# A hybrid recurrence and expert layer: the seam between a gated recurrence and a row projection rearranged (split early row, store awaited later, value splits placed sooner, four landing places)

## What is computed

```python
px = split(u_x @ w_in)                 # q, k, v, gate of group A; q, two z, v, gate of group B
ret = bidirectional_scan(q, k, v, fixed decays)          # group A: retention, 4 heads
f   = lb + (1 - lb) * sigmoid(z)                         # group B: HGRN2 recurrence, 4 heads
hg  = bidirectional_scan(silu(q), 1 - f, v, log f)
a = rms(ret) * silu(gate_a);  b = rms(hg) * w * silu(gate_b)
y = concat([a, b]) @ w_out
h = x + g1 * y                         # g1 and five other rows come from silu(c) @ w_ada + b_ada
out = rms(h + g2 * experts(...)) * norm_final_w
```

## Time and profile before

| what | us |
|---|---|
| time, median of three runs | 2895.38 |
| the profiled execution: its own time | 2889.01 |
| the profiled execution: span of the trace | 2887.3 |
| PE busy in the span | 2683.8 (93%) |
| DVE busy | 2034.6 (70%) |
| ACT busy | 1440.6 (50%) |
| mean granted TensorE clock | 0.965 of full speed |

### The profile page before, as it was taken

The page is one execution under the profiler, slowest core; times in us unless marked ns, Lnnn a source line. Parts: engine busy times, 40 slices in busy tenths (PEclk is TensorE's granted clock), DMA queues, the critical chain, the costliest instruction groups (busy, mean ns, idle before and its releaser), DMA issues. The chain is left out here.

```text
span 2887.3 us, 38466 instructions
## 1 busy us (share of the span) xinstructions
PE 2683.8 (93%) x13003; PEld 2124.9 (74%) x13004; DVE 2034.6 (70%) x2211; ACT 1440.6 (50%) x1471; POOL 510.9 (18%) x437
## 2 busy tenths in 40 slices
PE   7999999799679499999999999999999999999994
PEld 3668677477568387777787787888878877787773
DVE  3566666570666597899969878766686678967884
ACT  4433535320634375677747556544454446645653
POOL 0424434200002221112202111101111111111110
PEclk9999999899789699999999999999999999999997
DMA  6101100170233697899959878676586678968873
GB/s 254 30 23 30 30 23 15 65 257 1 95 117 83 245 351 264 283 360 358 362 197 350 297 243 315 229 251 201 189 285 203 215 269 298 343 204 278 283 242 131
DMA packets 266131, 596.65 MB, mean 207 GB/s; under 512 B 21356, under 2 KB 46612, under 8 KB 264944
## 3 DMA queue, kind: packets, MB, share of 16 engines
q1 hardware_dynamic: 245680, 552.56, 53.6%
q0 software_dynamic: 20384, 43.19, 6.7%
HBM read 577.75 MB, written 42.25 MB: 215 GB/s over the span
## 5 line engine op out<-in xcount | busy, mean ns | idle before, releaser
L2041 DVE TENSOR_TENSOR e_slot_r<-e_slot,whi 128x2048 fp32r<-128x2048 f32 x296 | 674.5, 2285 | 128.1 <-ACT whi L1983 128.1
L1983 ACT ACTIVATE whi<-e_slot 128x2048 fp32r<-128x2048 f32 x296 | 561.1, 1912 | 374.3 <-PE e_acc L1894 374.3
L1892 PE MATMUL e_acc<-whi,e_xhi 128*128 128x512 f32 x1600 | 631.3, 395 | 0.5
L1894 PE MATMUL e_acc<-whi,e_xlo 128*128 128x512 f32 x1600 | 628.4, 393 | 0.0
L1983 ACT ACTIVATE whi<-slot 128x2048 fp32r<-128x2048 f32 x148 | 283.1, 1913 | 186.2 <-PE e_acc L1894 186.2
L2041 DVE TENSOR_TENSOR slot_r<-slot,whi 128x2048 fp32r<-128x2048 f32 x151 | 345.0, 2287 | 19.9 <-ACT whi L1983 17.2
L1894 PEld LDWEIGHTS e_acc<-whi,e_xlo 128*128 128x128 f32 x1600 | 300.0, 187 | 70.6
L1892 PEld LDWEIGHTS e_acc<-whi,e_xhi 128*128 128x128 f32 x1600 | 301.1, 188 | 67.2 <-DVE e_slot_r L2041 4.2
L1892 PE MATMUL e_acc<-whi,e_ahi 128*128 128x512 f32 x800 | 320.4, 400 | 0.0
L1893 PE MATMUL e_acc<-slot_r,e_xhi 128*128 128x512 f32 x800 | 314.6, 393 | 0.0
L1894 PE MATMUL e_acc<-whi,e_alo 128*128 128x512 f32 x800 | 313.6, 392 | 0.0
(11 more groups left out here) (299 smaller groups left out, 3846.3 us busy)
## 6 DMA issues: line engine op xcount, KB each, us to landing
e_slot<-in_w SPq DMA_DIRECT2D x296, 1024.0 KB, 6.6
slot<-in_w SPq DMA_DIRECT2D x151, 1024.0 KB, 6.2
rv<-in_w_ada SPq DMA_DIRECT2D x32, 512.0 KB, 4.7
slot<-in_w_in SPq DMA_DIRECT2D x20, 512.0 KB, 4.1
wa<-in_w_ada SPq DMA_DIRECT2D x8, 1024.0 KB, 16.2
slot<-in_w_in SPq DMA_DIRECT2D x6, 1024.0 KB, 9.2
xt<-in_x SPq DMA_DIRECT2D x8, 512.0 KB, 16.9
slot<-in_w_out SPq DMA_DIRECT2D x4, 1024.0 KB, 14.1
```

Source lines behind the costliest of these rows:

```text
L1892: pe.matmul(out, hi[:, k, c], wh, start=False, stop=False)
L1894: return pe.matmul(out, lo[:, k, c], wh, start=False, stop=last)
L1983: act.activation(whi[i % RING][:], raw[i % PIECES][:], ACT.Copy).then_inc(S["whi_made"], 1)
L2041: v.tensor_tensor(wlo[i % PIECES][:], raw[i % PIECES][:], whi[i % RING][:].bitcast(F32), ALU.subtract).then_inc(S["wlo_made"], 1)
```

## The change

In `hgrn2`: `early_rows` takes the range of weight pieces to do. The last one is done in two halves on PE, with `output(h, 7)` between them; on ACT its copy moves behind `roots(h, 1)`. The buffer `o` is allocated ahead of `val` and `gate`. The store's semaphore becomes one that outlives the stage (`merged_out`), and the wait at the end of SP's list goes.

In `project_retention`: four landing places in place of five, one chunk further into `rv`, so that `rv` tiles 0 and 1 are free of them. ACT waits for the stores to have landed before it writes the high part of the second half of the value weights, and waits for the 32 adds ahead of value tile 2 in place of tile 0. DVE splits the value weights behind `low_rows(4)` and `low_rows(5)`.

```diff
+        o = t.sb("h_o", [P, LT, P])
         val = [t.sb(f"h_val{i}", [P, NT, P]) for i in range(2)]
         gate = t.sb("h_gate", [P, LT, P])
-        o = t.sb("h_o", [P, LT, P])
...
-                sp.dma_start(dram["merged"]..., o[:]).then_inc(S["o_out"], 16)
+                sp.dma_start(dram["merged"]..., o[:]).then_inc(keep["merged_out"], 16)
...
             store(HEADS - 2)
             store(HEADS - 1)
-            sp.wait_ge(S["o_out"], 16 * HEADS)
...
-            def early_rows(x):
+            def early_rows(x, which=range(KT)):
                 n = GROUPS * HEADS + x
-                if x < 2:
+                if which[0]:
+                    pass
+                elif x < 2:
                     group_read(pe, n - 2)
...
-                for k in range(KT):
+                for k in which:
...
-                mm.then_inc(S["rows_done"], 1)
+                if k == KT - 1:
+                    mm.then_inc(S["rows_done"], 1)
...
                 else:
-                    early_rows(3)
+                    early_rows(3, range(KT // 2))
                 if now:
                     output(h, LT - 1)
+                if not more:
+                    early_rows(3, range(KT // 2, KT))
...
                 if not more:
                     early_rows(2)
-                    early_rows(3)
...
                 if now:
                     roots(h, 1)
+                if not more:
+                    early_rows(3)
...
-                v.wait_ge(S["o_out"], 16 * h)
+                v.wait_ge(keep["merged_out"], 16 * h)
...
-        land = [keep["rv"][:]...[:, i * D:(i + 1) * D] for i in range(5)]
+        LANDS = 4
+        land = [keep["rv"][:]...[:, (i + 1) * D:(i + 2) * D] for i in range(LANDS)]
...
-                if n >= 5:
-                    sp.wait_ge(S["ada_added"], n - 4)
-                sp.dma_start(land[n % 5], ...).then_inc(ada_in[n % 5], 16)
+                if n >= LANDS:
+                    sp.wait_ge(S["ada_added"], n - LANDS + 1)
+                sp.dma_start(land[n % LANDS], ...).then_inc(ada_in[n % LANDS], 16)
...
-            for n in range(5):
+            for n in range(LANDS):
                 load_ada(n)
...
                 act.wait_ge(w_in[i], 16 * ((2 * n + half) // SLOTS + 1))
+                if (n, half) == (1, 1):
+                    act.wait_ge(keep["merged_out"], 16 * HEADS)
                 act.activation(whi[i][:], slots[i][:], ACT.Copy).then_inc(S["w_high"], 1)
...
-                if n == 1:
-                    act.wait_ge(S["ada_added"], CHUNKS)
                 if n == 2:
                     act.wait_ge(S["row_summed"], 1)
                 for i in range(first, end):
                     x = BASE[n] + i - first
+                    if n == 1 and i == 2:
+                        act.wait_ge(S["ada_added"], CHUNKS)
...
                 low_rows(i)
-                if i in (7, 8):
-                    low(1, i - 7)
+                if i in (4, 5):
+                    low(1, i - 4)
                 for _ in range(3):
                     add_ada(added)
```

More of the change, by code:

```diff
@@ L379, in hgrn2 @@
         cumulated keys_ready pool_sub exped dec_ready turned ktok_ready u_done states lev_sum lev_sub lev_exp lev_mul lev_ready s_done
-        picked st_ready o_done squared root_ready o_ready o_out rows_done rows_taken""".split()
+        picked st_ready o_done squared root_ready o_ready rows_done rows_taken""".split()
         S = {x: t.sem("h_" + x) for x in names}
@@ L413, in store @@
                 sp.wait_ge(S["o_ready"], LT * (h + 1))
-                sp.dma_start(dram["merged"].rearrange("(i p) n -> p i n", p=P)[:, :, (HEADS + h) * P:(HEADS + h + 1) * P], o[:]).then_inc(S["o_out"], 16)
+                sp.dma_start(dram["merged"].rearrange("(i p) n -> p i n", p=P)[:, :, (HEADS + h) * P:(HEADS + h + 1) * P], o[:]).then_inc(keep["merged_out"], 16)
             sp.dma_start(masks[:].rearrange("p a b -> p (a b)"), dram["masks"]).then_inc(S["const_in"], 16)
@@ L908, in project_retention @@
         acc = keep["rg"][:].rearrange("p i n -> p (i n)")
-        land = [keep["rv"][:].rearrange("p i n -> p (i n)")[:, i * D:(i + 1) * D] for i in range(5)]
-        ada_in = [t.sem(f"p_ada_in{i}") for i in range(5)]
+        LANDS = 4
+        land = [keep["rv"][:].rearrange("p i n -> p (i n)")[:, (i + 1) * D:(i + 2) * D] for i in range(LANDS)]
+        ada_in = [t.sem(f"p_ada_in{i}") for i in range(LANDS)]
         CHUNKS = 4 * KT
@@ L920, in load_ada @@
                 k, c = divmod(n, 4)
-                if n >= 5:
-                    sp.wait_ge(S["ada_added"], n - 4)
-                sp.dma_start(land[n % 5], wa[:, k, (2 + c) * D:(3 + c) * D]).then_inc(ada_in[n % 5], 16)
-            for n in range(5):
+                if n >= LANDS:
+                    sp.wait_ge(S["ada_added"], n - LANDS + 1)
+                sp.dma_start(land[n % LANDS], wa[:, k, (2 + c) * D:(3 + c) * D]).then_inc(ada_in[n % LANDS], 16)
+            for n in range(LANDS):
                 load_ada(n)
@@ L929, in _ @@
                 load_row_weights(sp, dram, keep, 1, half)
-            for n in range(5, CHUNKS):
+            for n in range(LANDS, CHUNKS):
                 load_ada(n)
@@ L1013, in add_ada @@
                 a = acc[:, c * D:(c + 1) * D]
-                v.wait_ge(ada_in[n % 5], 16 * (n // 5 + 1))
+                v.wait_ge(ada_in[n % LANDS], 16 * (n // LANDS + 1))
                 if k == 0:
-                    v.tensor_scalar(a, land[n % 5], sc[:, 0, k:k + 1], None, ALU.mult).then_inc(S["ada_added"], 1)
+                    v.tensor_scalar(a, land[n % LANDS], sc[:, 0, k:k + 1], None, ALU.mult).then_inc(S["ada_added"], 1)
                 else:
                     v.wait_ge(S["ada_added"], n - 3)
-                    v.scalar_tensor_tensor(a, land[n % 5], sc[:, 0, k:k + 1], a, ALU.mult, ALU.add).then_inc(S["ada_added"], 1)
+                    v.scalar_tensor_tensor(a, land[n % LANDS], sc[:, 0, k:k + 1], a, ALU.mult, ALU.add).then_inc(S["ada_added"], 1)
             low_rows(0)
@@ L2208, in build @@
             ident=m.sb("ident", [P, P]), const_in=m.sem("const_in"),
-            lb=m.sb("lb", [P, 8]), oml=m.sb("oml", [P, 8]), lb_ready=m.sem("lb_ready"), emptied=m.sem("emptied"), bound_part=m.sem("bound_part"), u_ready=m.sem("u_ready"), w_out_in=[m.sem(f"w_out_in{i}") for i in range(SLOTS)], hg_in=m.sem("hg_in"),
+            lb=m.sb("lb", [P, 8]), oml=m.sb("oml", [P, 8]), lb_ready=m.sem("lb_ready"), emptied=m.sem("emptied"), bound_part=m.sem("bound_part"), u_ready=m.sem("u_ready"), w_out_in=[m.sem(f"w_out_in{i}") for i in range(SLOTS)], hg_in=m.sem("hg_in"), merged_out=m.sem("merged_out"),
             w_in=[m.sem(f"w_in{i}") for i in range(PIECES)], nw_in=m.sem("nw_in"),
```

## The result

The changed kernel takes 2875.16 us (median of six runs, 2872.30 to 2880.13); the kernel before, run beside it, 2890.78 us (median of six). The ratio is 0.9946, with a 95% interval of 0.9935 to 0.9958: 15.6 us less, 0.54%. The forecast was 15.2 less; the three runs known then had a median of 2895.38, 4.6 above that of the six, so the forecast time of 2880.2 lies 5 us above the measured one, inside the range. The forecast gave 0.45 to more than 0.5% faster and 0.52 to less; 0.54% with an interval from 0.42 to 0.65 doesn't decide between the two.

A forecast was written before the change was run, and what follows sets the result against it. PE, busy for 93% of the span, was taken to set the pace. Gains of 3.44 + 2.79 + 8.93 = 15.16 us, taken from the three-run median of 2895.38, gave 2880.2 us; range 2869 to 2889.

The forecast's parts named there:

- Last output between the halves: End of the recurrence: the output starts sooner, with half of the last early row's products behind it; gain 3.44 us.
- Store awaited later: Boundary to the projection stage: first load 0.80 us behind the store's issue in place of 3.59; gain 2.79 us.
- Rival 2: Boundary to the projection: the barrier holds until the store has landed; gain 12.4 us, time 2883.0; chance 0.08.
- Value splits sooner: Projection's value weights: two PE pauses (5.4 us) and the slow clock behind them (about 3.5) go; gain 8.93 us.
- Rival 1: Behind the two value-weight pauses: the clock fall was that execution's own; gain 11.7 us, time 2883.7; chance 0.20.
- the pauses at 216 and 331: Two equal PE pauses of 2.21 us: clock stayed at 1.00 behind the first, fell to mean 0.62 behind the second.
- Rival 3: DVE late for `low_rows(5)`, 1.0 us of cover: a delay of 3 to 6 us gives 2881 to 2885; chance 0.09.
- Four places and later wait as guards: Projection's adds: they end near 636.2, PE wants them at 643.3, cover 7.1 us; protects the gain, adds none.
- Rival 4: Projection: four places starve the adds, slower than before; gain used up at 9.0 us per load; chance 0.03.
- Clock at the start: PE's slow stretch behind the seam, 5.6 us, worth 2.8: change between +1 and -1 us, taken as 0.
- Later stages: Stages behind the projection start at a barrier and move as a whole.
- Rival 5: Later stages' clock and DMA fall differently and take back 5 us or more: 2885 to 2890; chance 0.05.

The follow-up runs named there:

- e1: Kernel before with only the last output between the halves of the last early row and ACT's copy behind the root; 2886.94 us, ratio 0.9994.
- e6: Changed kernel with ACT's copy of the last early row back ahead of squares and root; one execution, 2879.65 us.
- e2: Kernel before with only the store awaited later, on a semaphore that outlives the stage; ratio 0.9993.
- e4: Changed kernel with the value splits back behind `low_rows(7)` and `low_rows(8)`; ratio 0.9978.
- e11: Changed kernel with both value splits behind `low_rows(4)`; one execution, 2878.19 us.
- e3: Kernel before with only the value splits behind `low_rows(4)` and `low_rows(5)`, keeping five landing places and the old wait; ratio 0.9990.
- e5: Changed kernel with two landing places in place of four; 2896.51 us, ratio 1.0024 against the kernel before.
- e12: Changed kernel with three landing places in place of four; one execution, 2880.60 us.
- e13: Changed kernel with high products first in the first tile, 8 idle PE products ahead of the projection's first wait, 6 more ending the recurrence; ratio 0.9960.
- e9: Changed kernel with 16 idle products on PE ahead of the projection's first wait; ratio 0.9948 against the kernel before.
- e10: Changed kernel with high products first in the first tile and 8 idle PE products ahead of the projection's first wait; ratio 0.9939.

## Why the prediction was right

- *Last output between the halves*: 3.44 expected, 3.43 in e1 and in the changed kernel. That ACT's move is needed holds (e6); that it is worth nothing by itself was not run. Its price if left out was 3.9, not 3.4, as the copy's own 0.6 us had been left out.
- *Store awaited later*: 2.79 expected, 2.82 measured. Rival 2, that the barrier holds until the landing, has fallen (e2). The 512 KB ahead of the first loads cost nothing: from the first load to the first product 5.34 us pass, before 5.35.
- *Value splits sooner*: 8.93 expected; e4 against the changed kernel gives 82.38 - 73.40 = 8.98. Rival 1, that the clock's 3.5 us were one execution's own, has fallen: eight pauses of eight in four profiles were followed by 0.50. The forecast's sum, not the lower bound from the pauses at 216 and 331, was right. The prediction had also weighed a mean gain inside the interval from 11.7 to 15.2; in these four profiles it lay at the upper end. Nor were the unequal ends of those two pauses mostly chance: in all 14 profiles the clock fell behind the one in the place of 331, and in 4 behind the one in the place of 216, so the place counts, and why stays open. Rival 3 did not happen, but its cover was 1.0 us as stated (e11); with that cover a delay of 3 us gives 2882, not the 2881 that the rival says.
- *Four places and later wait as guards*: the cover of the adds was put at 7.1 us and measured at 4.9, the adds ending 2.0 later, the end of "1 or 2". With five places and the old wait the gain of 8.9 falls to 1.7 (e3); the text had put the pause at 4.5 and was near (4.75), but named no slow clock behind it, which cost 2.5 more. Rival 4 needs 9.0 us a landing with four places; the median was 4.8 there and the longest 8.4. Its mechanism is real with two places (e5).
- *Clock at the start*: 0 expected, with 1 us either way. The slow stretch behind the seam measured 5.2 us against 5.6, worth 0.2.
- *Later stages* move as a whole: sum to retention is 73.6 in every kernel in which PE doesn't wait ahead of the sum, and from retention's first load to the end of the span it is 2161.4 us before and 2162.4 in the changed kernel (2160.3 to 2164.1 in all 14 profiles). Rival 5, that 5 us or more are taken back there, did not happen.

The sum of 15.16 meets 15.4 in the trace and 15.6 in the runs. It was written down from a median of three runs that stood 4.6 us above that of six, which is nearly all of the 5.0 by which the time itself is off.

## What to carry to other kernels

A wait at a stage's end for a store is free to move, if the buffer stays untouched until somebody checks the store's semaphore; the boundary itself cost 0.4 us here. A pause of PE in this stage cost more than its length, through the slow clock behind it: 3.5 us on top of the two pauses of 5.4, 2.5 on top of e3's 4.75, 1.7 on top of e12's 1.93. So placing a producer early enough that nobody waits for it paid 8.9 us for 5.4 us of pauses. But an earlier consumer moves every due time behind it, so list the next three. Here they were the reuse of the first bank, late by a pause of 4.75 us with the old wait (e3); the adds, with 4.9 us of cover left, which three places use up (e12); and `uT_r`, with 1.0, which both splits together use up (e11).

## What was not expected of the hardware

The same pause of about 2.2 us in the second head, with the same instructions in all kernels, ends with or without a fall of the clock. In the changed kernel's profile it fell (first PE's rows of this pause and of the same one a head later, then stretches with the columns as above, granted clock third from the right):

```profile
218.66 0.80 PE L537 MATMUL h_po<-h_val,h_st 128*128 128x128 f32 x2 [2.21 <-DVE h_st L828]
...
336.18 0.49 PE L537 MATMUL h_po<-h_val,h_st 128*128 128x128 f32 x2 [2.22 <-DVE h_st L828]
```
```profile
220.00:222.00 2.00, 2.00 (x5) 0.97 (x5) 2.00 (x3) 0.00 (x0) 0.59 (x1) 0.50 0.00 0
222.00:224.00 2.00, 2.00 (x4) 0.81 (x3) 1.97 (x3) 0.00 (x0) 2.00 (x1) 0.50 0.00 0
```

In that of e13 it didn't:

```profile
218.26 0.49 PE L537 MATMUL h_po<-h_val,h_st 128*128 128x128 f32 x2 [2.21 <-DVE h_st L830]
...
332.80 0.49 PE L537 MATMUL h_po<-h_val,h_st 128*128 128x128 f32 x2 [2.23 <-DVE h_st L830]
```
```profile
220.00:222.00 2.00, 2.00 (x6) 0.84 (x5) 1.97 (x4) 0.00 (x0) 0.98 (x1) 1.00 0.00 0
222.00:224.00 2.00, 2.00 (x6) 0.95 (x5) 2.00 (x2) 0.00 (x0) 1.91 (x1) 1.00 0.00 0
```

From there to the same pause of the next head 117.5 us pass in the one (218.66 to 336.18) and 114.5 in the other (218.26 to 332.80). Three of the profiles show the long form: the changed kernel (2880.13 us), e9 (2879.70) and e10 (2879.02), each 5 to 6.5 us above the median of its own runs. In e6's the clock fell too, a little later, and the stretch is 116.2 us. In the other ten, that of the kernel before among them, it stayed at full speed. The two pauses of 2.2 us that follow, in the third and fourth head, were followed by the fall in all 14. So 3 us of the 6.7 by which the two spans' difference falls short of 15.6 are this one pause. Another 1.95 had gone before the first product of the recurrence (57.81 before, 59.76 after, 57.8 to 60.2 in all profiles), and 1.0 behind retention's first load. The Trainium skill, "TensorE: Matmul & The Clock Gate", Part 1, says that the chip's watch on activity isn't reset when a kernel starts. The same pause with both endings in different executions agrees with that; that a pause a head later ends the same way in all 14 doesn't follow from it, and no run here shows what decides.
